# A two-model block on one core: the opening computed with features on partitions, its modulation in two feature halves

## What is computed

```
cond = silu(c)                                   # 1 x 1024
mod  = cond @ ada_w[l] + ada_b[l]                # 1 x 9216, nine vectors of 1024
sh1, sc1, g1, ... = split(mod, 9)
hn = rms_norm(h, norm_g[l,0]) * (1 + sc1) + sh1  # scale and shift by feature
h  = h + 0.5 * g1 * swiglu(hn, ffn1_w_in[l], ffn1_w_out[l])
```

## Time and profile before

| | |
|---|---|
| median of three runs | 2385.27 us |
| the profiled execution's own time | 2385.51 us |
| its span in the profile | 2383.8 us |
| mean granted TensorE clock | 0.979 |
| TensorE (PE) busy | 2280.7 us, 96% of the span |
| VectorE (DVE) busy | 1602.8 us, 67% |
| ScalarE (ACT) busy | 1124.5 us, 47% |
| first matmul of the loop of sub-block 0 | 62.69 us after the span's start |

### The profile page before, as it was taken

One profiled execution on the slowest core, in us unless ns is written; L12 is line 12 of the kernel. 1 busy time (PEld: TensorE's weight loads), 2 busy tenths in 40 slices (PEclk: granted clock), 3 DMA queues, 4 the chain that ended last, 5 costly groups with the idle time before them and its releaser, 6 DMA issues.

```text
span 2383.8 us, 31741 instructions
## 1 busy us (share of the span) xinstructions
PE 2280.7 (96%) x11796; PEld 1909.4 (80%) x11796; DVE 1602.8 (67%) x1813; ACT 1124.5 (47%) x1307; POOL 121.3 (5%) x174
## 2 busy tenths in 40 slices
PE   5999899999999999999999999999999999999998
PEld 3787787787788787688878889988888888998887
DVE  5886884777677687565565668686566556868655
ACT  2444454434444455444344366654445446665443
POOL 1000033000000004200000000000000000000000
PEclk9999998999999988999999999999999999999999
DMA  8896652687588473356555554446555555434553
GB/s 291 298 315 207 202 179 95 212 284 248 167 297 282 152 242 129 97 194 193 177 194 180 190 159 128 139 150 204 189 180 194 187 184 142 141 124 159 194 192 108
DMA packets 321381, 452.76 MB, mean 190 GB/s; under 512 B 32423, under 2 KB 269833, under 8 KB 320265
## 3 DMA queue, kind: packets, MB, share of 16 engines
q1 hardware_dynamic: 318232, 440.96, 56.3%
q0 software_dynamic: 2784, 9.50, 1.2%
q10 hardware_dynamic: 274, 1.06, 0.1%
HBM read 450.43 MB, written 1.05 MB: 189 GB/s over the span
## 4 chain that ended last, share of the span: by engine, by line
PE 85%; DVE 8%; ACT 3%; issue 2%; POOL 2%; POOLq 0%; DMA 0%; DVEq 0%; ACTq 0%
PE ps L558 19%; PE ps L560 19%; PE ps L559 19%; PE ps L551 4%; PE ps L552 4%; PE ps L553 4%; DVE wlo L1750 2%; PE ps L1038 2%; PE ps L662 1%; POOL side L2443 1%; PE ps L644 1%; PE ps L790 1%; PE ps L645 1%; PE ps L647 1%; PE ps L591 1%
## 5 line engine op out<-in xcount | busy, mean ns | idle before, releaser
L1750 DVE TENSOR_TENSOR wlo<-raw,whi 128x2048 fp32r<-128x2048 f32 (+1 forms) x348 | 791.6, 2278 | 396.2 <-ACT whi L1170 392.7
L1170 ACT ACTIVATE whi<-raw 128x2048 fp32r<-128x2048 f32 x346 | 660.0, 1910 | 282.3 <-PE ps L560 238.9
L558 PE MATMUL ps<-whi,xl 128*128 128x512 f32 x1472 | 593.6, 403 | 3.6 <-DVE u L1929 3.6
L560 PE MATMUL ps<-whi,xh 128*128 128x512 f32 x1472 | 575.2, 391 | 0.0
L559 PE MATMUL ps<-wlo,xh 128*128 128x512 f32 x1472 | 574.9, 391 | 0.0
L558 PEld LDWEIGHTS ps<-whi,xl 128*128 128x128 f32 x1472 | 277.2, 188 | 65.7 <-issue 4.8
L560 PEld LDWEIGHTS ps<-whi,xh 128*128 128x128 f32 x1472 | 277.1, 188 | 60.1
L559 PEld LDWEIGHTS ps<-wlo,xh 128*128 128x128 f32 x1472 | 277.5, 189 | 59.0 <-issue 4.8
L551 PE MATMUL ps<-xl,whi 128*128 128x256 f32 x864 | 254.4, 294 | 17.1 <-DVE wlo L1750 17.1
L558 PE MATMUL ps<-whi,hidl 128*128 128x512 f32 x640 | 252.2, 394 | 0.0
L560 PE MATMUL ps<-whi,hidh 128*128 128x512 f32 x640 | 249.2, 389 | 0.0
(11 more groups left out here) (375 smaller groups left out, 2553.6 us busy)
## 6 DMA issues: line engine op xcount, KB each, us to landing
raw<-in_ffn_w_in_dram SPq DMA_DIRECT2D x176, 512.0 KB
arena<-in_ada_w_dram SPq DMA_DIRECT2D x128, 512.0 KB, 5.7
raw<-in_w_in_dram SPq DMA_DIRECT2D x54, 1024.0 KB
raw<-in_ffn_w_out_dram SPq DMA_DIRECT2D x44, 1024.0 KB
raw<-in_w_ffn_gate_dram SPq DMA_DIRECT2D x88, 512.0 KB
raw<-in_w_ffn_up_dram SPq DMA_DIRECT2D x88, 512.0 KB
raw<-in_w_ffn_down_dram SPq DMA_DIRECT2D x44, 1024.0 KB
raw<-in_w_out_dram SPq DMA_DIRECT2D x16, 1024.0 KB
```

Of the source, the lines that this page charges most:

```text
L558: pe.matmul(o, al, wh, start=start, stop=False, **kw)
L560: return pe.matmul(o, ah, wh, start=False, stop=stop, **kw)
L1170: act.activation(whi[:, k % 3, :], raw[:, k % 3, :], ACT.Copy).then_inc(hi_done, 1)
L1750: tt(a[0], a[1], a[2].bitcast(F32), ALU.subtract).then_inc(lo_done, 1)
```

## The change

The opening is computed with features on partitions.

- `c`, `norm_g[0,0]` and the two `ada_b` pieces come as contiguous rows of 128 numbers (three loads); one transpose on TensorE turns all of them into `condT`. The broadcasting load of `norm_g` on GpSimd and the bias row on ScalarE's queue are gone.
- The 8 MB of `ada_w[0]` come as 16 half chunks of 512 KB (2 KB pieces), feature half f = 0 first, into six slots. Half chunks 2, 4 and 5 of the first half are reduced on TensorE (`mod_direct`: weights are the chunk, the moving operand is one column of `condT`, 8 float32 matmuls each); the other 13 on VectorE. `mod_sums(f)` adds VectorE's sum by 8 more one-column matmuls.
- Unit 0 is loaded after four half chunks, unit 1 after all 16.
- Tokens are scaled by their root alone (ScalarE, two copies of 128 x 1024), turned, and the turned tiles get scale and shift per partition (`x0`, ScalarE `Identity` with scale and bias). VectorE forms `xl`; the pass of TensorE that formed the rest is not used in sub-block 0.
- The first matmuls go by feature half for both token blocks (`first_turn`). `lo` of unit 2 moves ahead of the first products.
- The small parameters: 8 loads stay early, 16 (`lates`) go between unit loads late in sub-block 0. Their turning is split in three parts in the last two groups; masking `wsT` and the four scalings move to VectorE's end of sub-block 0.

```diff
-            for k in range(KC):                                    # SyncE
-                if k >= 3:
-                    sp.wait_ge(ada0_used, k - 2)
-                sp.dma_start(adaf[:, k % 3], ada0[k, :, 0:2048]).then_inc(ada0_loaded[k % 3], 16)
+            def ada_first(i):
+                if i >= 6:
+                    sp.wait_ge(*((ada0_summed, before0(i - 5, True)) if i - 6 in ON_PE else (ada0_used, before0(i - 5, False))))
+                sp.dma_start(adaf[:, i % 6], ada0[i % KC, :, i // KC, 0:2, :]).then_inc(ada0_loaded[i % 6], 16)
+            for i in range(4):
+                ada_first(i)
+            first_unit(0)
+            for i in range(4, 2 * KC):
+                ada_first(i)
+            first_unit(1)
...
+            def mod_direct(i):                                     # TensorE
+                f, k = divmod(i, KC)
+                pe.wait_ge(ada0_loaded[i % 6], 16 * (i // 6 + 1))
+                for at in range(KC):
+                    w = adaf[:, i % 6, at // 4, P * (at % 4):P * (at % 4) + P]
+                    ins = pe.matmul(ps[:, 6 + f, at:at + 1], w, condT[:, 0, k:k + 1],
+                                    start=(at == 0 and i == 2), stop=False, skip_group_check=True)
+                ins.then_inc(ada0_summed, 1)
+            mod_direct(2)
+            for a in range(2):
+                pe.wait_ge(xs_ready, 2 * a + 2)
+                for kc in range(KC):
+                    ins = pe.transpose(turned0(kc)[:, a * P:a * P + P], xs[:, a, kc * P:kc * P + P], ident[:, :])
+                ins.then_inc(xt_done, 2)
+            mod_direct(4)
+            mod_direct(5)
+            def first_turn(L):
+                for f in range(2):
+                    mod_sums(f)
+                    split_ready(L, f)
+                    ...    # 16 matmuls xh by wl and wh as xh comes, 8 xl by wh
...
+                act.wait_ge(root0_made, 1)                         # ScalarE
+                for a in range(2):
+                    act.activation(xs[:, a, :], h[:, a, :], ACT.Copy, scale=rstat[:, a, 1:2]).then_inc(xs_ready, 2)
                 hi(L, 0)
+                for f in range(2):
+                    act.wait_ge(mod_read, 2 * f + 2)
+                    for hh in range(2):
+                        ...    # two Identity 128x256 from PSUM, one Copy 128x512 to xh
+                    if f == 0:
+                        hi(L, 1)
+                hi(L, 2)
...
+            ada_first(0)                                           # VectorE
+            first_roots()
+            for i in (1, 3):
+                ada_first(i)
             def first():
+                lo(L, 0)
+                for i in range(6, KC + 2):
+                    ada_first(i)
+                mod_columns(0)
+                for i in range(KC + 2, KC + 5):
+                    ada_first(i)
+                rest_first(0, 0)
+                ada_first(KC + 5)
+                rest_first(0, 1)
+                for i in (KC + 6, KC + 7):
+                    ada_first(i)
+                mod_columns(1)
+                lo(L, 1)
+                for hh in range(2):
+                    rest_first(1, hh)
+                lo(L, 2)
...
                 lower_last(1)                                      # VectorE, end of sub-block 0
                 if n == 0:
                     dve.wait_ge(gate0_read, 2)
+                    dve.wait_ge(setup_kept, 3)
+                    tt(wsT[:, :, :], wsT[:, :, :], tri.unsqueeze(1).to_broadcast([P, 8, P]), ALU.mult)
+                    dve.wait_ge(late_loaded, LATES * 16)
+                    ...    # the scalings of dog and foxg
...
-            pool.dma_start(gain[:, :], norm_g[0, 0:1].rearrange("o d -> (o d)").partition_broadcast(P)
-                           ).then_inc(gain_loaded, 16)              # GpSimd, ahead of ident and drain
```

More of the change, by code:

```diff
@@ L304, in acc_ready, with before0 @@
                 eng.wait_ge(acc_done, 3 * n + 2 * a + f + 1)
+        ON_PE = (2, 4, 5)
+        def before0(i, pe):
+            return sum((k in ON_PE) == pe for k in range(i))
         TAPS = 2 * CONVK
@@ L434, in group @@
                             load(L, k0 + 4, whole(as2, k0 + 4, rows2(wd, l, i, GROUPS)), i)
+                            if n == 0 and two is None:
+                                setup_loads(2 if i else -1)
                             if tiles:
@@ L576, in turn_setup @@
[L576 to L583, removed]
+            pe.wait_ge(consts_ready, 1)
+            pe.wait_ge(cond_made, 1)
@@ new lines, in _, with mod_columns @@
+            pe.transpose(ps[:, 0, 0:4 * KC], cs[:, :], ident[0:4 * KC, 0:4 * KC]).then_inc(cond_turned, 1)
+            def mod_columns(f):
+                return [(4 * j + q, 1024 * j + 512 * f + P * q) for j in range(2) for q in range(4)]
+            def mod_direct(i):
[6 more added lines that the diff above has]
+                ins.then_inc(ada0_summed, 1)
@@ new lines, in _, with mod_sums @@
+            pe.wait_ge(ones_ready, 1)
+            def mod_sums(f):
+                pe.wait_ge(ada0_used, before0(KC * f + KC, False))
+                for at, col in mod_columns(f):
+                    ins = pe.matmul(ps[:, 6 + f, at:at + 1], acc[:, col:col + P], ones_col[:, 0:1], start=(f == 1 and at == 0),
+                                    stop=True, skip_group_check=True)
+                ins.then_inc(mod_summed, 2)
+            def first_turn(L):
+                pe.wait_ge(minus_ready, 1)
+                for f in range(2):
+                    mod_sums(f)
+                    split_ready(L, f)
+                    wh, wl = as4(whi, f), as4(wlo, f)
+                    for hh in range(2):
+                        pe.wait_ge(xh_ready, 2 * f + hh + 1)
+                        for a in range(2):
+                            for q in (2 * hh, 2 * hh + 1):
+                                kc, tok = 4 * f + q, slice(a * P, a * P + P)
+                                pe.matmul(ps[:, a, :], xh[:, kc, tok], wl[:, q, :], start=(kc == 0), stop=False)
+                                pe.matmul(ps[:, a, :], xh[:, kc, tok], wh[:, q, :], start=False, stop=False)
+                    pe.wait_ge(x_ready, 2 * f + 2)
+                    for a in range(2):
+                        for q in range(4):
+                            kc, tok = 4 * f + q, slice(a * P, a * P + P)
+                            ins = pe.matmul(ps[:, a, :], xl[:, kc, tok], wh[:, q, :], start=False, stop=(kc == KC - 1))
+                        if f == 1 and a == 0:
+                            ins.then_inc(gu_ready, 1)
+                    ins.then_inc(unit_used, 1)
@@ new lines, in turn_setup @@
+            def turn_setup(part):
+                if part == 0:
+                    pe.wait_ge(stage_loaded, STAGES * 16)
+                    pe.wait_ge(smalls_loaded, SMALLS * 16)
+                    for t, n in enumerate(STAGE_ROWS):
+                        ins = pe.transpose(ps[:, HT, t * P:t * P + n], stage[0:n, t, :], ident[0:n, 0:n])
+                else:
+                    for i in range(4):
+                        ins = pe.transpose(ps[:, (HT, MB)[part - 1], i * P:i * P + P], wsn[:, 4 * part - 4 + i, :],
+                                           ident[:, :])
@@ new lines, in first_roots @@
+            def first_roots():
+                dve.wait_ge(sq_ready, 4)
+                m, y, u = (rstat[:, :, i] for i in range(3))
+                two = ssq[:, :].rearrange("p (a f) -> p a f", a=2)
+                st(stt(m, two[:, :, 0], ROOT_W * EPS, two[:, :, 1], ALU.add, ALU.add))
+                st(ts(y.bitcast(I32), m.bitcast(I32), -0.5, ROOT_MAGIC, ALU.mult, ALU.add))
+                st(tt(u, y, y, ALU.mult))
+                st(tt(u, u, m, ALU.mult))
+                st(stt(y, u, -1.5 * ROOT_S, y, ALU.add, ALU.mult))
+                st(tt(u, y, y, ALU.mult))
+                st(tt(u, u, m, ALU.mult))
+                st(stt(u, u, -2.5 / ROOT_S ** 4, u, ALU.add, ALU.mult))
+                st(stt(y, u, 1.875 / ROOT_S, y, ALU.add, ALU.mult))
+                dve.sem_inc(root0_made, 1)
```

283 lines of the change are left out of this document (157 added, 126 removed).

## The result

The kernel after the change takes 2371.77 us (median of 5 runs, 2365.75 to 2375.22), the kernel before 2385.27 in the same comparison (5 runs): ratio 0.9943, 95% interval 0.9924 to 0.9961. That is faster by 13.5 us, where 12 were forecast. A second comparison gave 2369.36 against 2382.70, ratio 0.9943 [0.9923, 0.9963].

What follows compares the result with a forecast made beforehand. TensorE bounds the kernel after the first 63 us, so all gain was placed before the loop and at its clock: 11.7 + 2.8 - 1.1 - 1.4 = 12.0 us, from 2385.3 to 2373; range 2367 to 2381.

Steps and rivals of the forecast that it cites:

- Drain removed, `minus` near 4.5: Opening: without its load GpSimd's 5.447 us drain is short, so `consts_ready` comes at about 4.2, not 10.25.
- rival B: Opening: GpSimd's drain stays long, loop starts at 54, kernel takes 2376.5 us; chance 0.12.
- Loads: Opening: 0.4 MB a us from 2.6 on; half chunk 2 lands at 9.0, unit 0 at 12.9.
- rival C: Opening: each 512 KB load shows its own latency, one behind another; loop at 70, kernel 2392 us, slower; chance 0.03.
- One-column matmuls: Opening, TensorE: each `mod_direct` or `mod_sums` is 8 matmuls, 16 passes, 3.4 us a batch.
- p = 0.21: Opening, TensorE: time in us of one pass of a one-column matmul, taken at half clock.
- VectorE idle for 4 us before `mod_columns(0)`: Opening: VectorE waits 4 us for TensorE's `mod_sums(0)`, which ends at 25.9.
- The two halves: Before the loop: 24 matmuls per feature half, 7.9 us each, first half to 36.3, second to 50.0; loop starts at 51.0.
- Clock at the loop's start: Loop's start: TensorE idle under 1 us before it, so the clock stays at 2.4 GHz; 2.8 us gained.
- What comes back: After the loop's start: transposes 1.1 us and uncovered masking and scalings 1.4 lost; late loads taken as 0.
- rival E: Late in sub-block 0: late loads delay units or moved setup stalls the last groups; 3 to 9 us come back; chance 0.15.
- the stall before the loop: TensorE's 3.57 us idle ahead of the loop's start at 62.69; everything before the loop together was to win 11.7 us.

Runs made afterwards that it cites:

- e1: The kernel after with GpSimd's broadcasting load of `norm_g` put back ahead of the drain; loop's first matmul at 52.51, span 2370.0 us.
- e7: The kernel after with the 16 late loads issued behind the 8 early ones; loop's first matmul at 50.71, first residual 238.10, span 2378.8 us.
- e2: The kernel after with no half chunk on TensorE, all 16 on VectorE; loop's first matmul at 51.73, span 2373.6 us.
- e6: The kernel after with two half chunks (2 and 4) on TensorE, 5 on VectorE; loop's first matmul at 49.95, span 2368.2 us.
- e4: The kernel after with `wsT` masked on GpSimd and the four scalings moved into sub-block 1's mixer; loop to residual 178.02, span 2367.2 us.
- e8: The kernel before with only `hi` of unit 2 moved from the loop's head to between the first halves; loop at 59.44, span 2374.1 us.
- e9: The kernel after with masking on GpSimd, scalings moved, and 12 zero matmuls before the second half; median 2364.53 us, ratio to before 0.9925.
- e3: The kernel before with only GpSimd's broadcasting load moved behind the drain; loop's first matmul at 64.76, span 2382.9 us.

## Why the prediction was right, and where its terms were off

Forecast 2373, measured 2371.8. The step it stood on, that everything is won before the loop and at its clock, is shown by the anchors: 14.49 us at the loop's start; behind it the clock's 2.8 and what comes back cancel. The 14.5 of the forecast is another sum (11.7 at the loop's start and 2.8 of clock) and meets the measured 14.49 by chance. Set side by side: 11.7 forecast and 14.49 measured at the loop's start, 12.0 and 14.47 at the first residual. So the mechanism was right and the opening was undersized by 2.8 us; that the medians differ from the forecast by only 1.5 is partly luck, since the rest of the span moves by more than that. Point by point:

- *Drain removed, `minus` near 4.5.* Right in kind: 41 ns, `minus` at 3.71, and the load is what it waited for. But `cond_ready` comes near 7.5, not 5.3: the three rows, first in SyncE's queue and issued by 1.95, land near 6.2 (the sigmoid starts at 6.24), about when `x` does on the other queue, not by 4.0. Beside megabytes under way a small load didn't keep the 2.3 us that one took in a quiet stretch. The drain with its load is worth at most 2.0 us, the wait alone about nothing by the rows of e1, and nothing in the kernel before: rival B's 3.0 was too dear.
- *Loads.* Half chunk 2 at 10.27 (9.0), unit 0 at 14.53 (12.9), unit 1 at 35.05. I had reckoned 0.4 MB a us from 2.6 on. The windows up to 10 us add up to 2.9 MB, which is what that gives, and from 10 to 30 they moved 375 and 386 GB/s. So the bytes were right. The landings were 1.3 and 1.6 late, since I had let each load have the whole rate until it was in, one after the other; that loads under way together share it is my reading, and no run isolates it. Loads are close to a second bound: `lo` of unit 1 started at 37.20 and waited for `hi` alone, 0.24 us. The Trainium skill, "DMA: Bandwidth & Descriptors", section "Bandwidth", asks for 1 MiB or more a transfer; with several of 512 KB under way the trace shows next to no loss by that, 375 and 386 GB/s where the chunks of 1 MB moved 379 and 403 in the same windows of the kernel before, and rival C is refuted as a price. Its mechanism is there: SyncE waited 6.9 us for slots that TensorE held, and 10.3 in e7, where 284 GB/s were moved from 20 to 30 us; `lo` of unit 1 did not wait for a load there either.
- *One-column matmuls.* p = 0.21 was right for the first batch (3.54 us for 16, 0.22 with its end) and for `mod_sums(0)` (3.55). The 32 passes of half chunks 4 and 5 took 3.76, 0.117 each, where I had 6.8: the clock had risen. This is the largest mis-sized term, 3.0 us, of which TensorE's wait for VectorE takes 0.6 back. In e7, whose opening is otherwise the same, these passes fall on the low clock and the loop starts at 50.71, 2.5 later and next to the 51.0 forecast: the forecast's number is the slow one of two cases.
- *VectorE idle for 4 us before `mod_columns(0)`.* It was 1.13, and it is TensorE that waited for VectorE (0.62) at 21.50. With the passes at 0.117 VectorE and the loads are the bound there, not TensorE. e2 and e6 show it: each chunk taken from VectorE moves `mod_sums(0)`. With the slow passes it is TensorE, as forecast: VectorE waits 3.47 us in e1 and e7.
- *The two halves.* First half 27.43 to 34.66 (7.2; forecast 7.9), `mod_sums(1)` 1.84 (2.6), second half from 39.55 (forecast 42.1), 7.96 long as forecast. Last half chunk done at 34.5 (near 36). These are the other half of the error: 25.05 against 25.9 at the end of `mod_sums(0)`, then 0.7 less in the first half, 0.8 in `mod_sums(1)` at the high clock, 0.3 at the zeroing matmuls and 0.2 in small steps, 2.8 in all.
- *Clock at the loop's start.* Full from the first matmul, as forecast.
- *What comes back.* 1.4 us of mask and scalings, shown by e4, and ten transposes, 1.1 us by their rows; 0.3 is left unexplained of the 2.8 that the full clock brings (179.41 here against 176.62 in e8). Sum 2.5 forecast, 2.8 measured. The late loads cost 0 or that 0.3, and e7 shows that this hangs on their place (rival E's mechanism is real there).

So the 2.8 us by which the loop's start was off are what errors of both signs left. Too little was reckoned for the first loads (1.3 us), for TensorE's wait for VectorE (0.6) and for the transposes and `mod_sums(0)` (0.3); too much for the batch of 32 passes (3.0) and for everything behind `mod_sums(0)` (1.9). Close to half of the gain, 6.0 to 6.5, needed none of the turned layout (e8); in the forecast it was spread over two terms, the stall before the loop and the clock after it, without saying that one line carries both.

## What to carry to other kernels

Before taking a wait away in an opening that streams megabytes, lay the landing times of the loads beside it: the long drain was 5 us and worth nothing in the kernel before, where VectorE then ran into the loads, and by the rows about nothing in the kernel after; the load that it waited for may cost more there than the wait. An experiment that puts back a wait together with its load can't tell the two apart, and the rows can. A stall in front of a dense loop costs twice, itself and the half clock behind it, so look first for one instruction in the wrong place of a queue (6.0 to 6.5 of 14.5 us here). Read small effects at anchors inside the trace, since the rest of the span varied by 8.8 us from one execution to another.

## What the runs showed of the hardware

- A drain on GpSimd waits for a load that GpSimd has issued: 5.45 and 3.55 us with one under way, 41 ns with none.
- A float32 matmul of one column, 128 x 128 weights, costs two passes of 0.21 us at the low clock and 0.117 at the high one (`mod_sums(0)`, 3.55 us for 16 at a granted clock of 0.50, `mod_sums(1)`, 1.84 at 1.00). That is as much as a pass of a 128-column transpose, so between 1 and 128 columns the number of columns didn't matter; that the weights, the same in both, set the price is my reading.
- The clock rose during these passes in some executions and not in others of nearly the same program (32 passes in 3.76 or 6.83 us). The granted-clock column can't be used for it at the start: it reads 1.00 from 10 to 17 us in the kernel after, where passes are 0.21 apart as at 0.50 later, and in e9 it reads 1.00 through the first 58 us, although 512-column matmuls are 0.43 apart there from 30.98 to 36.7. Go by the distance of like matmuls there.
- `minus`, 128 x 128 on VectorE, takes 1.02 us in the kernel after, where GpSimd clears 128 x 1024 in the same us (3.70 to 4.65), and 0.23 in e3, where GpSimd clears nothing until 4.91. The Trainium skill, "SBUF — State Buffer", section "Terms", tells of a port that VectorE and GpSimd share and lock against each other; the trace agrees: `minus` ends at 4.73, just behind the clearing.
